# A hybrid attention block on one core: seven instructions of the block's attention section change places in three hand-written queues

## The reference

```python
h = rmsnorm(x, norm_g)
proj = h @ w_in
q_g, k_g, v_g, gk_lr, gate_g, u_p, gate_p, q_m, gate_m = split(proj)
gk = log_sigmoid(gk_lr @ w_gk_up + b_gk) / 16
o_gla = rmsnorm(gla_chunked(q_g, k_g, v_g, gk), gla_norm_g) * silu(gate_g)   # 4 heads, chunks of 64
o_pool = (multiscale_pool(u_p) @ pool_w) * pool_scale * silu(gate_p)
s = q_m @ k_mem.T * 64**-0.5                       # 4 heads, 256 memory tokens
o_mem = (softmax(s) @ v_mem) * silu(gate_m)
x = x + concat(o_gla, o_pool, o_mem) @ w_out
return rmsnorm(x, final_g)
```

## Time and profile before

| | us |
|---|---|
| median of 3 runs | 1554.27 |
| lowest and highest | 1553.05, 1554.46 |
| the profiled execution's own time | 1554.27 |
| its span, first to last instruction | 1552.8 |
| PE busy in the span | 1445.2 |

### The profile page before, as it was taken

How to read it: one execution, slowest core, us unless ns; L and a number is a source line. 1 busy time by engine, 2 the same in 40 slices (tenths; PEclk the granted TensorE clock), 3 DMA queues, 4 the chain that set the end, 5 groups by cost and what they waited for, 6 DMA issues and landing times.

```text
span 1552.8 us, 28261 instructions
## 1 busy us (share of the span) xinstructions
PE 1445.2 (93%) x11746; PEld 1045.8 (67%) x11746; DVE 724.4 (47%) x1221; ACT 607.9 (39%) x1101; POOL 236.1 (15%) x217
## 2 busy tenths in 40 slices
PE   3359699999999999999999999999999999999996
PEld 2238476776867677676867676686867667686762
DVE  2775635446162635436263544527163543716252
ACT  1344425344342524334252534434252534434241
POOL 1231201021210201121120202121020112111000
PEclk9679799999999999999999999999999999999997
DMA  8130100102020010102011010202001010201001
GB/s 335 65 136 1 41 2 28 54 0 81 0 81 1 27 54 14 68 0 81 0 42 39 27 54 0 81 0 81 0 27 54 17 64 0 81 0 44 12 28 68
DMA packets 15432, 69.32 MB, mean 45 GB/s; under 512 B 2352, under 2 KB 2480, under 8 KB 12848
## 3 DMA queue, kind: packets, MB, share of 16 engines
q1 hardware_dynamic: 15408, 68.98, 11.8%
HBM read 52.20 MB, written 16.78 MB: 44 GB/s over the span
## 4 chain that ended last, share of the span: by engine, by line
PE 82%; ACT 9%; DVE 4%; issue 2%; DMA 1%; POOL 1%; SPq 1%; ACTq 0%; DVEq 0%; POOLq 0%
PE bank L330 70%; ACT arena L728 2%; ACT arena L599 2%; PE bank L476 2%; PE bank L484 2%; PE bank L490 2%; PE bank L498 2%; DVE whl L852 1%; DVE arena L1013 1%; PE bank L541 1%; ACT L709 1%; PE bank L388 1%; ACT arena L738 1%; DMA whl<-in_pool_w 1%; PE bank L307 1%
## 5 line engine op out<-in xcount | busy, mean ns | idle before, releaser
L330 PE MATMUL bank<-arena,whl 128*128 128x256 f16 x6144 | 683.9, 274 | 3.0 <-DVE whl L852 3.0
L330 PEld LDWEIGHTS bank<-arena,whl 128*128 128x128 f16 x6144 | 602.1, 98 | 84.0 <-issue 6.3
L330 PE MATMUL bank<-arena 128*128 128x512 f16 x1536 | 344.1, 381 | 6.4 <-DVE arena L872 6.4
L330 PEld LDWEIGHTS bank<-arena 128*128 128x128 f16 x1536 | 148.4, 98 | 178.9 <-issue 13.1
L963 DVE SCALAR_TENSOR_TENSOR arena<-arena 64x256 f32<-64x256 f32 x60 | 25.2, 420 | 314.5 <-POOL arena L1191 313.1
L330 PE MATMUL bank<-whl,arena 128*128 128x512 f16 x768 | 168.3, 379 | 0.0
L686 ACT ACTIVATE arena<-bank,sca 128x512 f32<-128x512 f32 x64 | 43.9, 687 | 254.4 <-PE bank L330 253.3
L330 PEld LDWEIGHTS bank<-whl,arena 128*128 128x128 f16 x768 | 75.3, 99 | 86.9
L1143 POOL TENSOR_TENSOR arena<-arena 128x1024 f16<-128x1024 f32 x32 | 77.3, 2437 | 294.0 <-ACT arena L621 294.0
L1134 POOL TENSOR_TENSOR arena<-arena 128x1024 f32<-128x1024 f32 (+2 forms) x48 | 76.4, 1592 | 233.5 <-ACT arena L599 223.5
L1184 POOL TENSOR_TENSOR arena<-arena 128x542 f32<-128x542 f32 x16 | 17.4, 1089 | 605.2 <-ACT arena L693 598.3
(11 more groups left out here) (154 smaller groups left out, 1456.6 us busy)
## 6 DMA issues: line engine op xcount, KB each, us to landing
arena<-in_xt SPq DMA_DIRECT2D x16, 1024.0 KB, 5.2
arena<-in_x SPq DMA_DIRECT2D x32, 512.0 KB, 3.3
out<-arena SPq DMA_DIRECT2D x32, 512.0 KB, 2.6
arena<-in_w_in SPq DMA_DIRECT2D x8, 768.0 KB, 16.2
arena<-in_w_out SPq DMA_DIRECT2D x1, 4096.0 KB, 12.1
arena<-in_w_in SPq DMA_DIRECT2D x8, 392.0 KB, 16.4
arena<-in_w_mem SPq DMA_DIRECT2D x1, 2048.0 KB, 11.3
arena<-in_memt SPq DMA_DIRECT2D x1, 1024.0 KB, 6.9
```

Of the source, the lines that this page charges most:

```text
L330: mm = nc.tensor.matmul(ap, lhs, rhs, start=k == 0 and n == 0, stop=(k, n) == last)
```

## The change

Instructions trade places; none is added or removed. On PE, `turn_p(2)` moves ahead of `quarter(2)` (and so ahead of `rms_sum`). On ACT, the load of the table set moves ahead of the copy of `ket`, and `p_hi_of(3)` moves behind `norm_y(i-1, 0)`. On DVE, `p_norm(1)` moves ahead of `p_low(0)`, the maxima of units 2 and 3 move behind `state(0)` and `state(1)`, and `p_low(3)` moves behind `rows(1)`, `state(2)` and `pt_copy(1)`.

```diff
@@ PE @@
                 turn_p(1, 7)
+                pe.wait_ge(pt_out, 4 * i + 1)
+                turn_p(2, 6)
                 quarter(2)
                 if not last:
                     pe.wait_ge(p_exp, 4 * i + 4)
                     rms_sum(i + 1)
-                pe.wait_ge(pt_out, 4 * i + 1)
-                turn_p(2, 6)
                 pe.wait_ge(pt_out, 4 * i + 2)
                 turn_p(3, 7)
@@ ACT @@
                 silu(6, 3, 6)
+                nc.scalar.preload_act_table_set(EXP_LN)
                 act.wait_ge(pe_ket, i + 1)
                 if first:
                     act.wait_ge(lo_o, KT)
                 nc.scalar.activation(ket, bank[4][:, :].rearrange("p (a b c) -> p a b c", a=NT, c=DK),
                                      ACT.Copy).then_inc(ket_out, 1)
-                nc.scalar.preload_act_table_set(EXP_LN)
@@ ACT @@
                 p_hi_of(2)
-                p_hi_of(3)
                 if not first:
                     norm_y(i - 1, 0)
+                p_hi_of(3)
@@ DVE @@
                 p_norm(0)
+                p_norm(1)
                 p_low(0)
-                p_norm(1)
                 p_low(1)
                 rows(0)
+                state(0)
+                state(1)
                 mem_max(2)
                 mem_max(3)
-                state(0)
-                state(1)
                 pt_copy(0, 6)
                 p_norm(2)
                 p_norm(3)
                 p_low(2)
-                p_low(3)
                 rows(1)
                 state(2)
                 pt_copy(1, 7)
+                p_low(3)
                 state(3)
```

## The result

The changed kernel is slower, by about as much as was forecast:

| | before | changed |
|---|---|---|
| median, us | 1554.37 (4 runs) | 1582.70 (4 runs) |
| ratio of the two | | 1.0178, 95% interval 1.0158 to 1.0199 |
| profiled execution, own time | 1554.27 | 1580.85 |
| its span | 1552.8 | 1579.4 |

A forecast was written before the change was run, and what follows sets the result against it. PE, busy 93% of the span, was taken as the bound. 14 middle blocks x 2.01 us (0.24 + 1.77), +0.3 first, -0.3 last, gave 28.1 us: 1554.3 to 1582.4 us, range 1571 to 1594.

The forecast's parts named there:

- PE is the bound and any new wait is paid in full: PE, busy 93% of the span: a new wait costs in full unless a wait further down shrinks; none is left.
- The load ahead of the `ket` copy: ACT, ahead of quarter(0): PE waits 0.91 us a block, 0.24 net after the old turn_p(0) wait, inside the total.
- `p_norm(1)` earlier: DVE, ahead of p_low(0): fits in idle time, p_low(1) ends 1.13 us sooner.
- The upper bound's case: DVE: p_low(1) caught by POOL's folds loses 0.47 us; 2.48 a block, 35 us in all, 1589 us.
- `state` ahead of `mem_max`: DVE: state(0) and state(1) spend the 1.13 us gain, so mem_max(2) starts 0.09 us later.
- `turn_p(2)` ahead of `quarter(2)`: PE: turn_p(2) waits about 1.6 to 1.7 us for unit 2's chain; price 1.77 us a block.
- Unit 3 hidden: p_low(3) and p_hi_of(3) later: p_low(3) ends 1.6 us before turn_p(3) is due, so it costs nothing.
- First and last block: First block +0.3 us, at most 1, from the wait at turn_p(2); last block -0.3 us from an earlier output norm.
- The clock: Rival, chance 0.06: PE's clock falls in the new waits, 1.7 us more a block, 52 us in all, 1606 us.
- inert: Rival, chance 0.03: the order of the instructions is undone or has no effect, time unchanged.
- only the copy costs: Rival, chance 0.06: turn_p(2) doesn't wait, only the ket copy costs, 14 x 0.24 = 3.4 us, 1557.6 us.
- The faster side's number: Rival, chance 0.03: DVE's early reciprocal decides and the 0.67 us at turn_p(0) is won, 1545 us.

The follow-up runs named there:

- e6: The kernel before with quarter(1) ahead of turn_p(0) on PE, nothing else: 1544.48 us, ratio 0.9931.
- e2: The kernel before with only PE's move, turn_p(2) ahead of quarter(2): 1580.22 us, ratio 1.0164.
- e3: The changed kernel with the table load put back behind the ket copy: 1581.11 us, ratio 1.0170.
- e1: The changed kernel with PE's order put back, turn_p(2) behind quarter(2) and rms_sum: 1558.66 us, ratio 1.0026.
- e4: The kernel before with only the table load moved ahead of the ket copy: 1559.38 us, ratio 1.0028.
- e7: The changed kernel with p_hi_of(2) ahead of p_exp_of(3) on ACT and p_low(2) ahead of p_norm(3) on DVE: 1566.44 us, ratio 1.0072 to the kernel before.
- e5: The kernel before with only the new orders on DVE and of p_hi_of(3) on ACT: 1555.93 us, ratio 1.0002.
- e8: The kernel before with quarter(1) ahead of turn_p(0) except in the last block, where turn_p(2) goes ahead of quarter(2): 1543.38 us, ratio 0.9925.

## Why the prediction was right, step by step

- *PE is the bound and any new wait is paid in full.* Right. PE's busy time hardly moved (1445.2 to 1446.3), and the periods follow from its waits. Take the 87.81 us of the run without waits (`e6`) and add each wait and 0.16 us for it: the changed kernel comes to 90.48 (measured 90.49), `e2` to 90.40 (90.41), `e3` to 90.48 (90.49), `e1` and `e4` to 88.80 (88.81), `e7` to 89.40 (89.43). Only `e5` is off, by the 0.07 that its list of waits does not show.
- *The load ahead of the `ket` copy.* The order of events was right: load 0.71 after the start of `silu(6)`, `squares` where it was, 0.8 us of idle PE. The size was short: 0.24 net was forecast, two runs measured 0.33. The mis-sized term is the hand-over, which I took from `p_low` on DVE as 0.15 us; from the copy's end at 423.20 to the matmul at 423.44 it is 0.24. It lay inside the total, as forecast, so the time did not suffer; `e3` shows that it is inside.
- *`p_norm(1)` earlier.* Right: four `p_low` instructions in a row, 2.15 us from 428.80, which is the 1.35 and 0.80 forecast; `rows(0)` then starts 7.87 us after `squares`, forecast 7.90. The upper bound's case, `p_low(1)` caught by POOL's folds, did not come: they end at 429.86, and `p_low(1)` starts at 430.07.
- *`state` ahead of `mem_max`.* Right: `mem_max(2)` starts 9.76 after `squares` against 9.70 before, 0.06 late where 0.09 was forecast. The early reciprocal's gain is spent on the states, as `e5` confirms: no change alone.
- *`turn_p(2)` ahead of `quarter(2)`.* Right: the dear part. The period grew by 2.01 us, as summed; PE's move alone gives 1.93, forecast 1.92, and shortening the chain by 1.08 took 1.06 away. The idle time was 1.51, forecast 1.6 to 1.7, because PE arrived 0.09 later than I had it.
- *Unit 3 hidden.* Right in the changed kernel, with 442.35 + 0.15 against 444.44, 1.9 us of room. What I had not looked at was the same order without PE's move: there it misses by 0.07 us.
- *First and last block.* +0.3 and -0.3 were forecast, the profile shows 79.45 against 79.42 and 126.18 against 126.92, so +0.03 and -0.74. These are the poorest terms, and their error of 0.7 us is small beside what the start of the kernel differs from run to run (2.0 us over the ten profiles). What the forecast did not see is how the parts act in the last block. From its start to the end it is 126.9 us before, 124.7 with PE's move alone (`e2`), 125.4 with the new orders on DVE and ACT besides (`e3`) and 126.2 with the early load too. PE's move wins 2.2 us there, and the rest of the change takes most of it back. Each figure is from one profile, and the path by which the rest does so was not traced.
- *The sum.* 28.1 us forecast, 28.3 between the medians (28.2 without the long run), 26.6 between the profiled executions. So exact a hit is partly luck, as three runs of the changed kernel spread over 2 us; the middle blocks' share, 28.3 in the profile against 28.1, is not.
- *The rivals.* The clock did not fall: 1.00 in the block with both waits, and no middle block grew by more than 2.11 us, where a fall was priced at 1.7 on top of 2.01. Nor was the change inert: the load runs ahead of the copy. That only the copy costs is refuted in the changed kernel and is what `e1` looks like (1558.66, forecast for that case 1557.6). The faster side's number, 1545, was reached by `e6`, by another way: not by making the chain shorter but by putting 5.2 us of PE's own work ahead of the turn that waited for it.

Not tried: the first block by itself, and whether the 0.07 us of unit 3 would go with `p_hi_of(3)` back ahead of the norm.

## What to carry to other kernels

When one engine is busy without a break, look at every operation of its queue for how long ago its operands were ready. An operation whose operands come late wants independent work ahead of it: here moving 5 us of it away from `turn_p(2)` cost 1.9 us a block, and moving 5 us of it ahead of `turn_p(0)` won 0.67. Sum the chain over the other engines to the operand, compare it with the arrival of the busy engine, and take the larger; do not add up the delays, since an earlier wait on the busy engine is swallowed by a later one that hangs on another chain. And treat the last pass of a loop apart: there the same move alone won 2.2 us in the profiles of `e2` and `e8`, because another chain sets the end.

## What the runs showed of the hardware

- A wait of PE costs more than its idle time: eight transposes add 0.61 us to the chain behind a wait and 0.45 behind a busy PE, and hiding 0.51 us of idle time won 0.67. "Refill" is a name for these 0.16 us; no run shows what happens in them.
- The release of PE took 0.24 us from the end of the `ket` copy on ACT (423.20 to 423.44), and 0.15 us from the end of `p_low` on DVE (438.23 to 438.38). I had expected one number for both.
- DVE and POOL held each other up in a place that the change brought together. In the changed kernel the product with the pooling gate (line 1085) took 2.54 us while POOL formed the low half of the next x:

```profile
451.34 4.66 POOL L1143 TENSOR_TENSOR arena<-arena 128x1024 f16<-128x1024 f32 x2 [21.47 <-ACT arena L621]
451.48 2.54 DVE L1085 TENSOR_TENSOR arena<-arena 128x512 f32<-128x512 f32 x1
453.94 0.74 DVE L1087 SCALAR_TENSOR_TENSOR arena<-bank,sca,arena 128x512 f32<-128x512 f32 x1
```

  In the kernel before the same product took 0.68 at 448.33, beside the same two instructions of POOL (446.28 to 450.99). Over the whole run, before and then changed (busy us, mean ns of one):

```profile
L1085 DVE TENSOR_TENSOR arena<-arena 128x512 f32<-128x512 f32 x16 | 16.9, 1059 | 0.0
L1085 DVE TENSOR_TENSOR arena<-arena 128x512 f32<-128x512 f32 x16 | 36.0, 2252 | 0.0
```

  That is 19.1 of the 22.4 us by which DVE's busy time grew. In every middle block of these two traces the length goes with who comes first. In the changed kernel POOL's instruction starts 0.11 to 0.30 us ahead of the product, which takes 2.38 to 2.57 us in all 14. Before, POOL's second instruction is the one that meets it: in 11 blocks the product starts 0.02 to 0.20 us ahead of that and takes 0.68 to 0.79, in 3 it starts 0.02 to 0.03 us behind and takes 2.65 or 2.66. The Trainium skill (SBUF — State Buffer, "SBUF: two separate sides") gives the mechanism, a lock held for a whole instruction by whichever starts first; no run here tested it by itself. It cost nothing in the changed kernel, as `quarter(3)` ran on PE until 455.4.
- The table load ahead of the `ket` copy takes 1.28 us, starts 0.02 us after the activation ahead of it has ended, and lets the next one start 0.01 us after itself (421.31 + 1.28 = 422.59, 422.60). The Trainium skill (ScalarE: Activation LUTs, "What ACT_TABLE_LOAD costs") adds some 1.38 us for a drain to every switch; no row here shows it.
